# Router logits taken from the sum ahead of its norm, and the second tile's norm put on ScalarE and GpSimd

## The reference, cut to what matters

```python
h_lat = _post_norm(h_lat, m_lat[2] * y_lat, ln_mix_g[layer], ln_mix_b[layer])   # layer_norm(4**0.25 * h + branch)
f_lat = _expert_choice_ffn(_modulate(h_lat, m_lat[3], m_lat[4]), w_router[layer], ...)   # u = h * (1 + scale) + shift
...
logits = jnp.einsum('bnd,de->ben', u, w_router)      # in the ffn
aff = jax.nn.softmax(logits, axis=1)                 # over the experts
gate, idx = lax.top_k(aff, cap)                      # 32 tokens for each expert
ye = silu(xe @ w_g) * (xe @ w_u) @ w_d * gate        # xe: the chosen rows of u
h_lat = _post_norm(h_lat, m_lat[5] * f_lat, ln_ffn_g[layer], ln_ffn_b[layer])
```

## Time and profile before

| | |
|---|---|
| median of 3 runs | 2175.22 us (2172.39 to 2175.73) |
| profiled execution | 2164.6 us, its span 2162.8 us |
| PE, PEld, DVE, ACT, POOL busy | 81%, 47%, 27%, 17%, 3% of the span |
| weight stream, expert groups | 428 GB/s |
| bytes read from HBM | 583.96 MB |

### The profile page before, as it was taken

The page is one execution under the profiler, slowest core; times in us unless marked ns, Lnnn a source line. Parts: engine busy times, 40 slices in busy tenths (PEclk is TensorE's granted clock), DMA queues, the critical chain, the costliest instruction groups (busy, mean ns, idle before and its releaser), DMA issues. The chain is left out here.

```text
span 2162.8 us, 26649 instructions
## 1 busy us (share of the span) xinstructions
PE 1743.1 (81%) x11816; PEld 1024.9 (47%) x11816; DVE 565.7 (26%) x1119; ACT 359.5 (17%) x725; POOL 54.2 (3%) x73
## 2 busy tenths in 40 slices
PE   6897765656568977756566589999999999999999
PEld 4454221111117842211111177776578678775785
DVE  1434010001007640100000035422353143413532
ACT  2231100000000011000000013323431122324310
POOL 0000000000000000000000001010000001100000
PEclk9998888888779988787888899999999999999999
DMA  9994999999999959999999943212423332213220
GB/s 405 380 381 168 423 428 429 427 427 428 428 428 425 377 184 422 428 428 428 427 428 428 428 171 118 73 62 88 156 79 117 126 118 80 74 64 120 114 105 32
DMA packets 43809, 586.71 MB, mean 271 GB/s; under 512 B 4944, under 2 KB 5072, under 8 KB 8112
## 3 DMA queue, kind: packets, MB, share of 16 engines
q1 hardware_dynamic: 40752, 573.80, 64.4%
q0 software_dynamic: 2224, 8.48, 1.0%
q10 hardware_dynamic: 720, 2.74, 0.3%
HBM read 583.96 MB, written 1.05 MB: 270 GB/s over the span
## 5 line engine op out<-in xcount | busy, mean ns | idle before, releaser
L1333 PE MATMUL ps<-arena 128*32 128x512 f32 x1536 | 242.2, 761 | 152.9 <-DMA arena<-in_experts 150.4
L1333 PE MATMUL ps<-ring,arena 128*32 128x512 f32 x1504 | 239.5, 767 | 149.5 <-DMA ring<-in_experts 147.2
L1103 PE MATMUL ps<-arena,ring 128*128 128x256 f32 (+3 forms) x1184 | 234.8, 359 | 6.1 <-DVE arena L1923 2.6
L1103 PEld LDWEIGHTS ps<-arena,ring 128*128 128x128 f32 (+2 forms) x1184 | 202.1, 189 | 36.1 <-ACT arena L696 6.1
L1333 PEld LDWEIGHTS ps<-arena 128*32 128x32 f32 x1536 | 49.0, 125 | 309.7 <-DMA arena<-in_experts 170.7
L1333 PEld LDWEIGHTS ps<-ring,arena 128*32 128x32 f32 x1504 | 48.5, 125 | 309.7 <-DMA ring<-in_experts 171.0
L1437 PE MATMUL ps<-arena,ring 128*128 128x256 f32 x768 | 188.8, 391 | 0.0
L1437 PEld LDWEIGHTS ps<-arena,ring 128*128 128x128 f32 x768 | 141.1, 191 | 29.8 <-issue 10.0
L1460 PE MATMUL ps<-arena,ring 128*128 128x256 f32 x640 | 152.7, 389 | 0.0
L1460 PEld LDWEIGHTS ps<-arena,ring 128*128 128x128 f32 x640 | 121.7, 193 | 31.3 <-issue 15.4
L1103 PE MATMUL ps<-arena 128*128 128x256 f32 (+2 forms) x480 | 102.5, 374 | 6.1 <-ACT arena L998 2.5
(11 more groups left out here) (343 smaller groups left out, 1848.6 us busy)
## 6 DMA issues: line engine op xcount, KB each, us to landing
arena<-in_experts SPq DMA_DIRECT2D x96, 2048.0 KB, 35.9
ring<-in_experts SPq DMA_DIRECT2D x94, 2048.0 KB, 35.9
ring<-in_stream SPq DMA_DIRECT2D x61, 2048.0 KB, 8.4
arena<-in_stream SPq DMA_DIRECT2D x15, 2048.0 KB, 21.3
ring<-in_stream SPq DMA_DIRECT2D x2, 1728.0 KB, 7.1
gate<-in_b_mod POOLq DMA_DIRECT2D x4, 512.0 KB, 10.8
ln<-in_experts SPq DMA_DIRECT2D x2, 1024.0 KB, 5.2
tab<-in_experts SPq DMA_DIRECT2D x2, 1024.0 KB, 7.7
```

The source lines that it names most:

```text
L1103: mm = M(dst, lhs(k), rhs(k), start=k == 0, stop=k == n - 1)
L1333: mm = M(bank(b + half)[32 * e:32 * e + 32], x[:, k, 32 * e:32 * e + 32], wk(e, half), start=k == 0, stop=k == KD - 1, tile_position=(0, 3 ...
```

## The change

The logits no longer wait for h. With t the sum ahead of the norm, mu its mean and rs one over its deviation, u = (t - mu) rs g (1 + scale) + b (1 + scale) + shift. So the logits are rs (t W') plus a row that is the same for all tokens:

- `router_weights` (VectorE, after attention and after the convolution) makes W g (1 + scale) and W (b (1 + scale) + shift), and their sums over k. A product with ones in `mix_out`, between its tiles, sums these over the partitions into bank 4. `router_norm` subtracts a 1024th of the column sums from the first, which takes the mean out of every product, and copies the row of the second.
- TensorE transposes t as soon as each half's sum is there; ScalarE copies three halves and VectorE the fourth, plainly, 512 columns at a time; logits of the tiles go to banks 0 and 1. VectorE scales them by rs and adds the row into `ff["ex"]`, which the softmax now reads.
- rs comes from Ln and Exp on ScalarE, with their table set loaded at the start, and not from Sqrt and a reciprocal.
- Tile 0's norm stays on VectorE. Tile 1's is put behind the exponentials: ScalarE makes (t - mu) rs in h, then GpSimd multiplies by the gain and adds the bias. The first gather waits for both tiles' h.
- WHOLE is now chunk 8 and waits for ScalarE's centred tile; HALVED is chunk 9 and waits for GpSimd's last pass. What waited for chunk 8 on GpSimd (the next norm parameters) waits for chunk 9.
- The second norm of each layer (after the experts) is as it was.

```diff
@@ -42,7 +42,7 @@
...
-HALVED, WHOLE = WIDE, WIDE + 1
+WHOLE, HALVED = WIDE, WIDE + 1
...
@@ -162,6 +162,8 @@
...
             col(f"b_mod{layer}{m}", None if b is None else b[m * D:(m + 1) * D], KD)
+        for n in ("ln_mix_g", "ln_mix_b"):
+            col(f"{n}{layer}", sub(f(n), layer), KD)
...
@@ -446,12 +448,16 @@
...
-        pn = dict(t=ff["acc"], st=sc.take(24, TT), mv=sc.take(4, TT), rs=sc.take(4, TT))
+        pn = dict(t=ff["acc"], st=sc.take(24, TT), mv=sc.take(4, TT), rs=sc.take(6, TT))
...
+        route_t = tab2[:, n_first:n_second + 1024]
+        o = KD * 2 * E
+        rt = dict(w=route_t[:, 0:o].rearrange("p (k e) -> p k e", k=KD), gain=route_t[:, o:o + KD], lift=route_t[:, o + KD:o + 2 * KD],
+                  sum=route_t[:, o + 2 * KD:o + 2 * KD + 2 * E], row=route_t[:, o + 2 * KD + 2 * E:o + 2 * KD + 3 * E])
...
@@ -645,12 +651,12 @@
...
-                        sp.wait_ge(*S("post_dve").at("h", layer, 0, 1))
+                        sp.wait_ge(*S("post_pool").at("h", layer, 1))
...
-                            sp.wait_ge(*S("ffn_pe").at("logits", layer))
+                            sp.wait_ge(*S("post_act").at("centered", layer))
...
@@ -754,12 +760,33 @@
...
+            def router_norm(l):
+                Sa, Sv, Sp = S("post_act"), S("post_dve"), S("route_pe")
+                nc.scalar.preload_act_table_set(LN_EXP)
+                def deviation(a):
+                    act.wait_ge(*Sv.at("var", l, 0, a))
+                    A(pn["rs"][:, a, 0:1], pn["mv"][:, a, 1:2], ACT.Ln, bias=T1("eps")).then_inc(*Sa.up("log", l, 0, a))
+                    act.wait_ge(*Sa.at("log", l, 0, a))
+                    A(pn["rs"][:, a, 1:2], pn["rs"][:, a, 0:1], ACT.Exp, scale=-0.5).then_inc(*Sa.up("sd", l, 0, a))
+                deviation(0)
+                for a, half in ((0, 0), (0, 1), (1, 0)):
+                    act.wait_ge(*Sp.at("turned", l, a, half))
+                    A(ff["ut"][:, 4 * half:4 * half + 4, a * P:(a + 1) * P], bank(4 + 2 * a + half).rearrange("p (k n) -> p k n", k=4),
+                      ACT.Copy).then_inc(*S("route_act").up("ut", l, a, half))
+                deviation(1)
...
-                    A(ff["ex"][:, a], bank(0)[:, a * E:(a + 1) * E], ACT.Exp, bias=ff["st"][:, 2 + a:3 + a],
+                    A(ff["ex"][:, a], ff["ex"][:, a], ACT.Exp, bias=ff["st"][:, 2 + a:3 + a],
...
+                act.wait_ge(*S("post_dve").at("shift", l))
+                A(h[:, 1], pn["t"][:, 1], ACT.Identity, scale=pn["rs"][:, 1, 1:2], bias=pn["rs"][:, 1, 2:3]
+                  ).then_inc(*S("post_act").up("centered", l))
...
@@ -1257,6 +1284,9 @@
...
                             mm.then_inc(*S("mix_pe").up("out", l, j))
+                    if a == 0:
+                        pe.wait_ge(*S("route_dve").at("sum", l))
+                        M(bank(4, 2 * E), T1("ones"), rt["sum"], start=True, stop=True).then_inc(*S("route_pe").up("sum", l))
...
@@ -1298,15 +1328,21 @@
...
                 Sa, Sp, Sv = S("ffn_act"), S("ffn_pe"), S("ffn_dve")
-                pe.wait_ge(*loaded("router", l + 1))
-                router = small_t[:, 512:640].rearrange("p (k e) -> p k e", k=KD)
+                Sr, t = S("route_pe"), pn["t"]
+                pe.wait_ge(*S("route_dve").at("row", l))
                 for a in range(TT):
-                    turn(f"ffn{l}", h, a, lambda a: S("post_dve").at("h", l, 0, a))
-                    turned(f"ffn{l}", a)
-                    if a == 0:
-                        pe.wait_ge(*S("post_dve").at("weighed", l, 0, 0, 1))
-                    mm = project(bank(0)[:, a * E:(a + 1) * E], lambda k: ff["ut"][:, k, a * P:(a + 1) * P], lambda k: router[:, k])
-                mm.then_inc(*Sp.up("logits", l))
+                    for half in range(2):
+                        pe.wait_ge(*S("post_dve").at("sum", l, 0, a, half))
+                        for k in range(4 * half, 4 * half + 4):
+                            mm = nc.tensor.transpose(bank(4 + 2 * a + half)[:, k % 4 * P:k % 4 * P + P], t[:, a, k * P:(k + 1) * P],
+                                                     T1("ident"))
+                        mm.then_inc(*Sr.up("turned", l, a, half))
+                for a in range(TT):
+                    for half in range(2):
+                        pe.wait_ge(*S("route_dve" if a and half else "route_act").at("ut", l, a, half))
+                        for k in range(4 * half, 4 * half + 4):
+                            mm = M(bank(a, E), ff["ut"][:, k, a * P:(a + 1) * P], rt["w"][:, k, 0:E], start=k == 0, stop=k == KD - 1)
+                    mm.then_inc(*Sp.up("logits", l, a))
...
@@ -1346,6 +1382,9 @@
...
+                    if g == 0:
+                        pe.wait_ge(*S("post_dve").at("h", l, 0, 0))
+                        pe.wait_ge(*S("post_pool").at("h", l, 1))
...
@@ -2017,33 +2056,85 @@
...
+            def router_weights(l):
+                Sr = S("route_dve")
+                router = small_t[:, 512:640].rearrange("p (k e) -> p k e", k=KD)
+                g, b = (par[:, par_at[f"{n}{l}"][0]:par_at[f"{n}{l}"][0] + KD] for n in ("ln_mix_g", "ln_mix_b"))
+                wide = lambda ap: ap.unsqueeze(2).to_broadcast([P, KD, E])
+                ve.wait_ge(*loaded("router", l + 1))
+                ve.wait_ge(*S("mod_dve").at("columns", l, 3))
+                V.tensor_tensor(rt["gain"], g, modcol[:, l, 3, :, 0], ALU.mult).then_inc(*Sr.up("gain", l))
+                V.tensor_tensor(rt["lift"], b, modcol[:, l, 3, :, 0], ALU.mult).then_inc(*Sr.up("scaled", l))
+                ve.wait_ge(*Sr.at("scaled", l))
+                V.tensor_tensor(rt["lift"], rt["lift"], modcol[:, l, 2, :, 0], ALU.add).then_inc(*Sr.up("lift", l))
+                ve.wait_ge(*Sr.at("gain", l))
+                V.tensor_tensor(rt["w"][:, :, 0:E], router, wide(rt["gain"]), ALU.mult).then_inc(*Sr.up("w", l, 0))
+                ve.wait_ge(*Sr.at("lift", l))
+                V.tensor_tensor(rt["w"][:, :, E:2 * E], router, wide(rt["lift"]), ALU.mult).then_inc(*Sr.up("w", l, 1))
+                ve.wait_ge(*Sr.at("w", l, 1))
+                V.tensor_reduce(rt["sum"], rt["w"].rearrange("p k e -> p e k"), AX_X, ALU.add).then_inc(*Sr.up("sum", l))
+            def router_norm(l, ready):
+                Sv, Sr, Sa = S("post_dve"), S("route_dve"), S("post_act")
+                ve.wait_ge(*S("route_pe").at("sum", l))
+                V.scalar_tensor_tensor(out=rt["w"][:, :, 0:E], in0=bank(4, E).unsqueeze(1).to_broadcast([P, KD, E]), scalar=-1.0 / D,
+                                       in1=rt["w"][:, :, 0:E], op0=ALU.mult, op1=ALU.add).then_inc(*Sr.up("centered", l))
+                V.tensor_copy(rt["row"], bank(4, 2 * E)[:, E:2 * E]).then_inc(*Sr.up("row", l))
+                ve.wait_ge(*loaded("ln", 4 * l + 2))
+                if l == 0:
+                    ve.wait_ge(*loaded("x"))
+                for a in range(TT):
+                    for half in range(2):
+                        k = (l, 0, a, half)
+                        cols = slice(half * HALF, (half + 1) * HALF)
+                        t = pn["t"][:, a, cols]
+                        ve.wait_ge(*ready(a, half))
+                        V.tensor_tensor(t, bank(2 * a + half), gate[:, 0, cols], ALU.mult).then_inc(*Sv.up("weighed", *k))
+                        ve.wait_ge(*Sv.at("weighed", *k))
+                        V.scalar_tensor_tensor(out=t, in0=h[:, a, cols], scalar=ALPHA, in1=t, op0=ALU.mult, op1=ALU.add
+                                               ).then_inc(*Sv.up("sum", *k))
+                        ve.wait_ge(*Sv.at("sum", *k))
+                        V.bn_stats(pn["st"][:, a, 6 * half:6 * half + 6], t).then_inc(*Sv.up("stats", *k))
+                    ve.wait_ge(*Sv.at("stats", l, 0, a, 1))
+                    V.bn_aggr(pn["mv"][:, a], pn["st"][:, a]).then_inc(*Sv.up("var", l, 0, a))
+                    mv, rs = pn["mv"][:, a], pn["rs"][:, a]
+                    if a == 0:
+                        ve.wait_ge(*Sv.at("var", l, 0, a))
+                        V.scalar_tensor_tensor(out=h[:, a], in0=pn["t"][:, a], scalar=mv[:, 0:1], in1=ln[:, 0], op0=ALU.subtract,
+                                               op1=ALU.mult).then_inc(*Sv.up("gained", l, 0, a))
+                        ve.wait_ge(*Sa.at("sd", l, 0, a))
+                        ve.wait_ge(*Sv.at("gained", l, 0, a))
+                        V.scalar_tensor_tensor(out=h[:, a], in0=h[:, a], scalar=rs[:, 1:2], in1=ln[:, 1], op0=ALU.mult, op1=ALU.add
+                                               ).then_inc(*Sv.up("h", l, 0, a))
+                ve.wait_ge(*S("route_pe").at("turned", l, 1, 1))
+                V.tensor_copy(ff["ut"][:, 4:KD, P:T], bank(7).rearrange("p (k n) -> p k n", k=4)).then_inc(*Sr.up("ut", l, 1, 1))
+                ve.wait_ge(*Sa.at("sd", l, 0, 1))
+                V.scalar_tensor_tensor(out=pn["rs"][:, 1, 2:3], in0=pn["mv"][:, 1, 0:1], scalar=-1.0, in1=pn["rs"][:, 1, 1:2],
```

(21 more changed lines are left out.)

33 lines of the change are left out of this document (13 added, 20 removed).

## The result

| | before | after |
|---|---|---|
| median of 4 runs | 2173.8 us (2170.2 to 2175.73) | 2154.41 us (2153.48 to 2157.55) |
| ratio | | 0.9915, 95% interval 0.9897 to 0.9933 |
| profiled execution, its span | 2164.6, 2162.8 us | 2153.72, 2151.9 us |

The change is faster, by 0.85%. The forecast gain was 13.0 us; this first comparison shows 18.5 us (0.0085 of 2173.8), the pair of profiled executions 10.9. Which of the three is right, and through which steps it comes, took the experiments to say.

A forecast was written before the change was run, and what follows sets the result against it. The first block was taken as bound by its weight stream, with dips at two router stages. Gains of 6.6 and 6.7, less 0.3, made 13.0; 2164.6 became 2151.6, plus 10.6 carried over 2162.2, range 2158 to 2170.

The forecast's parts named there:

- The step that failed: Whole execution: profiled 2164.6 lies 10.6 below the runs' median 2175.22; that difference was added to 2151.6, giving 2162.2.
- The low end: Whole execution: shorter passes and centring give a gain of 14.2, 2161.0; less a scatter of 2.8, 2158.
- The sum of 13.3: Both router stages: chunk 10 lands 6.6 us earlier in layer 0 and 6.7 in layer 1.
- The start of the softmax: Router stage: row maximum 6.1 us behind the last weighing instead of 13.4, 7.15 us earlier.
- ScalarE's centring: Second tile's norm, behind the exponentials: ScalarE centres 128x1024 in 1.3 us, bounds 0.6 and 2.4.
- GpSimd's passes: Second tile's norm, behind the centring: two passes over 128x1024 at 3.25 us each.
- VectorE beside GpSimd: Softmax to picks: two operations with two SBUF inputs, scan and rank times chosen, stretch by nothing to 1.3 us together.
- Which side decides: Chunk 10's arrival: the DMA side sets it; the gather frees chunk 0 by 208.8, HALVED is in at 209.9.
- What should cost nothing: Router's folded weights, 4.1 us, fit VectorE's 4.35 us wait; first tile's later start is covered by 3.5 us.
- Rival 1: Layer 0, GpSimd's first arithmetic: code setup is exposed, one layer's gain is lost, 2168.5 us; chance 0.12.
- Rival 2: Router logits: TensorE's clock falls all the same, 3.8 us per layer, gain 5.4, 2169.8 us; chance 0.08.
- Rivals 3 and 4: GpSimd's two passes: stretched to 6.4 us each, 2174.6, chance 0.09; or 9.75 each, slower, 2188, chance 0.05.

The follow-up runs named there:

- swap back: The changed kernel with HALVED as chunk 8 and WHOLE as chunk 9 again: median 2159.37 us, ratio 0.9941.
- pool longer: The changed kernel with one more 128x1024 pass on GpSimd ahead of its two, into a buffer nothing reads there: 2157.47 us, one run.
- vec fit: The changed kernel with the second tile's norm back on VectorE, laid into its waits, GpSimd idle there: median 2154.37 us, ratio 0.9930.
- before warm: The kernel before with nine unread products per router stage, meant to keep TensorE's clock up: median 2170.55 us, ratio 1.0009.

## Why the prediction missed, point by point

**The step that failed** is the last: "That execution lies 10.6 below the median of the runs shown, 2175.22; the stages do not tell why, so I carry the difference over". The forecast was low in gain by 1.2 (13.0 against 14.2, plus or minus 2.1) and high in its base by 5.8 (2175.22 against the mean of 2169.4), so the base is what took it out of the range. The median of three happened to be that of high ones: only 3 of all 63 executions lie above 2175.22, and one equals it. The mean of the 63 lies 4.8 above the profiled 2164.6, not 10.6. With it the same sum gives 2156.4, which is 2.0 above the median measured. The low end had the same flaw: "the runs shown scatter 2.8 below their median" took three runs for the scatter, where 63 span 15.4 us. Why these three were high stays open.

**The sum of 13.3** (6.6 and 6.7) came out, but partly by luck, since errors of opposite sign in its terms nearly cancel (below). Chunk 10 is in at 35.19 behind w on average over ten stages of before and at 28.5 over six of after: 6.7 per stage, 13.4 per execution; of these the stretch keeps 12.7. That the landing decides is borne out by swap back (+6.8 at the landings, +5.9 in the stretch), pool longer (+4.3, +3.1), vec fit (-1.8, -3.1) and before warm, where chunk 10 landed as in the kernel before and neither stretch nor time moved. Outside w to landing the two kernels agree within 0.5 us in every part, as shown above.

**The start of the softmax.** Forecast 6.1 behind w, measured 5.92 in five of six stages. 32 logit instructions took 3.64 (forecast 3.8), the ones-product 0.30 on TensorE (0.15), the copies from PSUM were hidden. The clock stayed up in all but the last microsecond of one stage.

**ScalarE's centring.** Forecast 1.3, measured 1.23; the table load came behind it.

**GpSimd's passes.** Forecast 3.25 each, measured 2.33 and 2.34. I doubled the 1.54 and 1.71 of the earlier trace rows. Those two ran beside VectorE's operations with two inputs, in the rows themselves, and were longer for it or hold a part that does not grow with the size; no run parts the two. A smaller form in the kernel before, 128x256, speaks for the first, as 0.73 is less than a third of 2.33:

```profile
L2592 POOL TENSOR_TENSOR arena<-arena,tab 128x256 f32<-128x256 f32 x20 | 14.5, 727 | 50.1 <-PE ps L1547 25.7 <-PE ps L1510 24.4
```

HALVED was therefore issued at w + 13.1 and not w + 15.1. The Trainium skill (GPSIMD Engine Reference, 3.1 Elementwise — side-by-side cycle accounting) gives 4497 ns for an addition of two 2048-element inputs. Half of that, 2.25, is an estimate for 1024 elements from that page; the trace agrees, 2.33.

**VectorE beside GpSimd.** Forecast: scan and the product behind it stretched by up to 1.3. Measured: the scan and the product were not stretched, as they start behind GpSimd's end, but the compare ahead of them, which has one input, went from 0.28 to 1.04. The Trainium skill (GPSIMD Engine Reference, 8. Key points) says that the two engines contend where VectorE has two SBUF inputs or a 2-port mode. The rows of the changed kernel and of pool longer agree for the scan, which has two SBUF inputs, and show how: the held instruction goes on until GpSimd's running one ends. The compare has one input; that it runs in a 2-port mode no row shows.

**Which side decides.** I wrote "the DMA side decides, and the gather has over a microsecond of cover". That was wrong: the shorter passes brought the end of the extra chunks' bytes to w + 20.1, where I had w + 21.8, and chunk 10 was issued at w + 20.4, so the picks decide by a little. Chunk 10 then met DMA engines that had run dry, and needed 7.6 to 7.9 us where I had counted 4.9 behind a running stream. These two errors have opposite signs, 1.7 and 2.8. But the 2.8 is not all a cost of the pause, since 4.9 is a rate and 7.7 a time from issue to landing. By landings alone, HALVED's last half is in at w + 21.6 to 22.7 in the six stages of after and chunk 10 5.6 to 6.8 behind it, where a stream without a pause takes 4.9: the pause costs 0.7 to 1.9. The landing of chunk 10 came at 28.5 where I had 26.7; before it was at 34.7 by the same view where I had 33.4, which takes 1.3 of the 1.8 away again, since both levels were read from the DMA engines' rates and not from landings. Two things more pull at the picks' side: the compare's 0.76, and the first expert products at 1.2 GHz.

**What should cost nothing** did cost nothing that shows: VectorE was through with tile 0 at 180.10, 6.4 us ahead of w, and w of layer 0 is no later on average (188.2 against 188.4). The terms that the prediction adds up there end at 182.0, not at 182.3, which changes nothing.

**Rival 1**, a wait for GpSimd's code in layer 0, did not happen: the first pass starts 0.15 us behind ScalarE's end (193.43 + 1.23 = 194.66, start 194.81), and the one in layer 1 likewise at 783.14. **Rival 2** showed in one of six stages and for 0.4 us. **Rivals 3 and 4** fell with the passes of 2.33 us.

## What to carry to other kernels

Where an offload costs another engine nothing by its own queue, look at what runs beside it: here GpSimd was done 2.2 us ahead of its deadline and still held the engine that set it, and the same work laid into VectorE's own waits was as fast. A difference at the place that sets the pace (here, when one chunk lands), averaged over five and three traces, gave the effect within a microsecond (13.4 against 14.2). One pair of traces did not: its landings gave 11.8 and its stretch 9.1, and the ratio of two medians of four gave 18.5. And a median of three is a weak base for an absolute time: here it sat 5.8 us above the mean of 63.
